# Modulation sums moved from VectorE to GpSimd, with a shorter expert choice and another order of the filling blocks, in a fused two-block kernel

## The chip, the cores and the metric

One Trainium2 chip (trn2), one of its cores. The metric is the device time in microseconds of one execution; lower is better. The kernel before took 1738.4 us, the median of 3 runs (1738.04 to 1740.64).

## What is computed

256 tokens (SEQ), width 1024, float32 throughout. The first block has four layers, each with another mixer; every layer is modulated by a condition vector `c`:

```python
cond = jax.nn.silu(c)
for i in range(DEPTH):                      # 4 layers: gla, sgu, fox, gla
    mod = (cond @ w_mod[i] + b_mod[i])[:, None, :]
    shift, scale, gate = jnp.split(mod, 3, axis=-1)
    h = rms_norm(x, norm_pre_g[i]) * (1.0 + scale) + shift
    o = mixer(h)                            # w_in, mixing, w_out
    x = x + gate * rms_norm(o, norm_post_g[i])
```

The second block adds a hybrid mixer (three attention groups, a convolution, gates) and then the PEER feed-forward: for each token and each of 8 heads the 16 best of 128 x 128 experts, found from two sets of 128 scores, whose rows of `expert_down` and `expert_up` are gathered from HBM:

```python
top_s, top_i = lax.top_k(s, 16)             # per head: 16 best keys of each of two sets
best_s, pos = lax.top_k(cand_s, 16)         # of the 256 sums
idx = jnp.take_along_axis(cand_i, pos, axis=-1)          # expert number, key0 * 128 + key1
a = gelu(einsum('cd,ced->ce', x, expert_down[idx]))
y = einsum('ce,ced->cd', softmax(best_s) * a, expert_up[idx])
```

## The kernel before, in words

The tokens are two tiles of 128 (t = 0 and 1). All engines run one list, `ORDER`, which `make_order` writes out: each engine walks it and does its share of every step, so an engine that waits at a step holds everything behind it on that engine. The steps of tile 0 set the order. A `"gap"` in the lists of chunks stands where tile 0 has to wait for a chain of small work; the next block of tile 1 is put there to fill TensorE. A block is one `("mm", t, name, i)`: 8 matmuls of 128x512 (line 948) from 2 MB of weights that SP loads into a ring of four 1 MB places. Tile 1 is behind tile 0 and its last layers run beside the expert gathers of tile 0.

**Modulation.** A layer's shift, scale and gate are three vectors of 1024. `w_mod` of a layer is read in 24 pieces of 128x1024 (three thirds of KC = 8 pieces). The piece, times one column of `cond`, is added to a running sum of 128x1024; afterwards a matmul with ones adds up the 128 partitions. `PIECES` lists the 96 pieces. Pieces 0 to 15 (shift and scale of layer 0) are loaded by SP at the start, two at a time, into `early`. Six of them (`PE_PIECES`) are done by TensorE itself in `piece_columns` (line 986), the other ten by VectorE in `add_piece` (line 1567). The other 80 come over GpSimd's queue (`fetch`, line 849) into the four places of `mring`, and VectorE adds each of them at a `("mod", n)` step; `pieces_at` says how many such steps stand behind each block. `start_sums` (lines 856 and 857) clears the three sums of a layer and loads the bias, `fetch_post` loads `norm_post_g`. There are two sets of sums, for even and odd layers.

The sums are read by TensorE at `mod_cols` of a layer (line 1010: 8 matmuls for the shift and 8 for the scale, before the layer's first block) and at `mod_gate` (line 1019, behind the fifth and sixth block of the layer). The evacuation of the first block of layer 3 by ScalarE waits for all 96 pieces, since its target lies where `mring` and the sums lie.

**The start.** TensorE: `piece_columns` of pieces 5 and 7, the transposes of both tiles (line 927), `piece_columns` of pieces 9, 11, 13, 15, then `mod_cols` 0, then the first block.

**Fox layer** (layer 2): eight blocks; `forget_sum` (line 1100), `quad_T` (line 1111), `quad_S` (line 1123) are the steps behind its blocks 3 and 4. After the output projection of each of the layers there are two filling blocks.

**Experts.** `choose` makes the 16 picks of a head on VectorE (lines 1732 to 1781). 256 picks in all (PICKS), 128 per tile; a `("tick", k)` gathers the rows of pick k on GpSimd (line 877), takes the dot product with the down row on VectorE (line 1798) and adds the weighted up row of an earlier pick: on VectorE (line 1813) or, through a diagonal matrix made by ScalarE (line 1493), on TensorE (line 1203). `on_vector` says which; `added_at` says at which tick: 18 ticks behind the pick in tile 0 and 6 in tile 1. The weights of tile 1's picks are made in groups of four (`GROUPS`, `weights`, line 1790). `final` adds the two sums and normalizes.

## Time and profile before

| | before |
|---|---|
| median of 3 runs | 1738.4 us (1738.04 to 1740.64) |
| profiled execution, its own time | 1739.41 us |
| span of the profiled execution | 1737.6 us |
| TensorE busy | 1393.7 us, 80% |
| VectorE busy | 1047.5 us, 60% |
| ScalarE busy | 433.1 us, 25% |
| GpSimd busy | 490.7 us, 28% |
| HBM read | 589.55 MB, mean 340 GB/s |

The profile is one execution. Its span lacks 1.8 us of that execution's own time, and that time is 1.0 us above the median. Busy shares are averages over stages which have different limits, so they are read by stage: the layers (0 to about 800 us), the time in which tile 1's layers run beside tile 0's gathers (to about 1390 us), and the gathers of tile 1.

### The profile page before, as it was taken

To read this page: it belongs to the slowest core of one execution; us is meant where nothing else is said; L and a number is where in the kernel's file an instruction comes from. 1 tells how busy PE (TensorE), PEld (TensorE's weight loads), DVE (VectorE), ACT (ScalarE), POOL (GpSimd) and SP (SyncE) were. 2 spreads that over 40 slices of the span, in tenths; PEclk is the share of its full clock that TensorE was granted. 3 is DMA by queue.
4 is the path that set the end of the run, shared out by engine and by line. 5 is a ranking of instruction groups with operands and counts; after the bars stand their busy time and mean duration, and the time that the engine had idled before them with its cause. 6 is when DMAs were issued, how large, how long until landed. Compare 5 with 4: busy or idle time off the path is not lost. (4 is left out here: it accounts for less than half of the span.)

```text
span 1737.6 us, 13867 instructions
## 1 busy us (share of the span) xinstructions
PE 1393.7 (80%) x4158; PEld 717.6 (41%) x4158; DVE 1047.5 (60%) x2197; ACT 433.1 (25%) x974; POOL 490.7 (28%) x498
## 2 busy tenths in 40 slices
PE   6998988978999999999777777699787647666665
PEld 6454435444444455444354343455333312222222
DVE  3645554553233222313797998788866778877876
ACT  1221413423423421102133232132002221111111
POOL 2101210210000000000445546355344545444441
PEclk9998998989999999999897888798888878898898
DMA  9978884978556776887999989999999999999995
GB/s 386 377 256 303 312 340 171 347 282 295 213 207 219 277 265 242 290 293 265 402 361 357 413 339 403 412 400 413 410 414 414 348 412 422 421 422 421 422 421 248
DMA packets 108941, 591.53 MB, mean 340 GB/s; under 512 B 12450, under 2 KB 12706, under 8 KB 60612
## 3 DMA queue, kind: packets, MB, share of 16 engines
q0 software_dynamic: 67776, 312.56, 45.4%
q1 hardware_dynamic: 41092, 278.10, 42.2%
q8 instruction: 34, 0.56, 0.1%
q14 instruction: 39, 0.32, 0.0%
HBM read 589.55 MB, written 1.05 MB: 340 GB/s over the span
## 5 line engine op out<-in xcount | busy, mean ns | idle before, releaser
L948 PE MATMUL bank<-ring,hT 128*128 128x512 f32 x1888 | 866.6, 615 | 39.6 <-DVE room L1920 12.1
L948 PEld LDWEIGHTS bank<-ring,hT 128*128 128x128 f32 x1888 | 366.5, 198 | 482.2 <-issue 449.8
L877 POOL DMA_INDIRECT room<-in_peer_down,idx x92 | 102.5, 1114 | 525.1 <-DVE idx L1781 401.8
L1798 DVE CUSTOM_DVE_ANT_0 room<-room 128x1024 f32<-128x1024 f32 x180 | 218.6, 1221 | 50.6 <-DMA room<-in_pair,idx 38.4
L1203 PE MATMUL bank<-room 128*128 128x512 f32 x284 | 150.9, 676 | 96.5 <-ACT room L1493 94.2
L1813 DVE SCALAR_TENSOR_TENSOR x<-room,pcoef,x 128x1024 f32<-128x1024 f32 x121 | 155.7, 1287 | 28.0 <-DMA room<-in_peer_up,idx 27.5
L877 POOL DMA_INDIRECT room<-in_peer_up,idx x104 | 114.0, 1096 | 88.6 <-DVE pa L1798 42.3
L1203 PEld LDWEIGHTS bank<-room 128*128 128x128 f32 x284 | 57.5, 215 | 190.8 <-issue 97.2
L849 POOL DMA_DIRECT2D room<-in_w_mod x80 | 42.2, 528 | 326.3 <-DVE room L1567 206.5
L877 POOL DMA_INDIRECT room<-in_pair,idx x88 | 97.0, 1102 | 108.5 <-PE bank L1203 50.6
L927 PE MATMUL bank<-cst,room 128*128 128x128 f32 x424 | 64.7, 297 | 55.3 <-ACT room L1439 24.1
L1203 PE MATMUL bank<-ring,room 128*128 128x512 f32 x116 | 72.6, 774 | 38.0 <-ACT room L1493 38.0
L1567 DVE SCALAR_TENSOR_TENSOR room<-room,cst 128x1024 f32<-128x1024 f32 x58 | 74.4, 1282 | 36.0 <-DMA room<-in_w_mod 26.8
L927 PEld LDWEIGHTS bank<-cst,room 128*128 128x128 f32 x424 | 54.9, 153 | 82.4 <-ACT room L1439 26.8
L964 PE MATMUL bank<-room 128*128 128x128 f32 x256 | 43.9, 331 | 34.7 <-DVE room L1592 34.7
L1493 ACT ACTIVATE room<-cst,pcoef 128x128 f32<-128x128 f32 x102 | 36.8, 392 | 118.0 <-DVE pcoef L1790 110.8
L1439 ACT ACTIVATE room<-room,anm 128x128 f32<-128x128 f32 (+1 forms) x80 | 35.4, 443 | 116.3 <-DVE anm L2004 116.3
L877 POOL DMA_INDIRECT ring<-in_pair,idx x40 | 46.6, 1166 | 61.8 <-PE bank L1203 30.8
L1798 DVE CUSTOM_DVE_ANT_0 ring<-ring,room 128x1024 f32<-128x1024 f32 x40 | 48.8, 1226 | 23.1 <-DMA ring<-in_pair,idx 22.8
L1203 PEld LDWEIGHTS bank<-ring,room 128*128 128x128 f32 x116 | 26.7, 243 | 80.6 <-ACT room L1493 52.3
L964 PEld LDWEIGHTS bank<-room 128*128 128x128 f32 x256 | 40.0, 236 | 44.9 <-DVE room L1592 40.1
L1272 ACT ACTIVATE room<-bank 128x512 f32<-128x512 f32 x24 | 14.3, 596 | 147.0 <-PE bank L948 147.0
(304 smaller groups left out, 1527.4 us busy)
## 6 DMA issues: line engine op xcount, KB each, us to landing
ring<-in_wpk SPq DMA_DIRECT2D x248, 1024.0 KB, 7.0
room<-in_w_mod POOLq DMA_DIRECT2D x80, 512.0 KB, 8.2
room<-in_w_mod SPq DMA_DIRECT2D x8, 1024.0 KB, 15.8
room<-in_norm_post_g POOLq DMA_DIRECT2D x4, 512.0 KB, 5.0
rowb<-in_gate_bias SPq DMA_DIRECT2D x4, 512.0 KB, 9.0
room<-in_peer_up,idx POOLq DMA_INDIRECT x104, 12.5
room<-in_peer_down,idx POOLq DMA_INDIRECT x92, 12.4
room<-in_pair,idx POOLq DMA_INDIRECT x88, 14.3
```

Of the source, the lines that this page charges most:

```text
L849: pool.dma_start(mring[n % 4], w[:, k, third * D:(third + 1) * D]).then_inc(S(f"pool_in{n % 4}"), 16)
L877: return pool.indirect_dma_start(out=dst, out_offset=None, in_=A[table][0] if table != "pair" else A[table], in_offset=bass.IndirectOffset ...
L927: last = tr(cols4(b, i), src(i), ident)
L948: last = mm(bank[p][:, :], lhs, ring[:, h % 4, k * N:(k + 1) * N], start=(kk == 0), stop=(h == halves[-1] and k == 3))
L964: last = mm(cols4((b, c, a)[l % 3], h), k_[:, h * P:(h + 1) * P], q_[:, h * P:(h + 1) * P], start=True, stop=True)
L1203: last = mm(bank[WORK[tile][i]][:, :], diag[:, nth % 4, :], row[:, i * N:(i + 1) * N], start=(v == mine[0]), stop=(v == mine[-1]), skip_gr ...
L1272: af(dst, src, ACT.Copy).then_inc(done, 1)
L1439: last = af(s, s, ACT.Exp, bias=anm[:, t, n, h:h + 1], accum_out=al[:, t, n, h:h + 1])
L1493: af(diag[:, nth % 4, :], ident, ACT.Copy, scale=pcoef[:, v // TOPK % 4, v % TOPK:v % TOPK + 1]).then_inc(S("diag"), 1)
L1567: v.scalar_tensor_tensor(out=a, in0=piece, scalar=const("cond", k, 1), in1=a, op0=ALU.mult, op1=ALU.add).then_inc(S("summed"), 1)
L1798: v.tensor_tensor_reduce(out=row, in0=row, in1=u_(g // MINE), scale=1.0, scalar=0.0, op0=ALU.mult, op1=ALU.add, accum_out=pa[:, g // TOPK ...
L1813: v.scalar_tensor_tensor(out=x[:, tile, :], in0=row, scalar=pcoef[:, w, e:e + 1], in1=x[:, tile, :], op0=ALU.mult, op1=ALU.add) \
```

## The change

It does seven things.

1. The 80 pieces behind layer 0's shift and scale (`POOL_PIECES`) are multiplied and added by GpSimd, in two instructions each (a tensor_tensor in place in `mring`, and one into the sum), and the `("mod", n)` steps and `pieces_at` are gone. GpSimd adds one piece after the other, four loads ahead, and counts them in `pool_summed`; TensorE's and ScalarE's waits for pieces are now waits for that count. The first load waits until VectorE has done its part of the first 16.
2. Of the first 16 pieces TensorE does two (5 and 7), VectorE fourteen.
3. The fox layer has a filling block behind its block 3, and only one behind its output projection.
4. In tile 0's query projection the transpose and the scores of the first two heads stand one block earlier, and so does `choose` 0.
5. `choose` has fewer instructions: the two casts to float go, the pairs of comparisons, products and sums are one instruction each, and the last product writes the integer index itself.
6. The last eight picks' up rows are added two to a tick, the last group of four weights is two groups of two, and VectorE and TensorE share these rows otherwise; four ticks fewer.
7. The semaphores `wsT` and `gqk` are one, `dve_set`.

```diff
 def out_chunks(t, L):
     return [([("gated_T", t, L)], ("mm", t, f"out{L}", 0), [("post0", t, L)]),
             ([], ("mm", t, f"out{L}", 1), [("post1", t, L)]),
-            "gap twice"]
+            "gap" if L == 2 else "gap twice"]
...
             b(3, [], [("unit", t, 1), ("forget_sum", t)]),
+            "gap",
             b(4, [], [("quad_T", t, 0), ("quad_S", t, 0)]),
...
-            b(0, name="query", pre=[("norm_in", t, 5)]),
-            b(1, [("score_T", t, 0)], name="query"),
-            b(2, [("score_S", t, 0), ("score_T", t, 1)], name="query"),
+            b(0, [] if t else [("score_T", t, 0)], name="query", pre=[("norm_in", t, 5)]),
+            b(1, [("score_T", t, 0)] if t else [("score_S", t, 0)], name="query"),
+            b(2, ([("score_S", t, 0)] if t else []) + [("score_T", t, 1)], name="query"),
...
-TICKS = PICKS + REST + LEAD[1]
-PIECES = [(L, third, k) for L in range(DEPTH) for third in range(3) for k in range(KC)]
-
-PE_PIECES = (5, 7, 9, 11, 13, 15)
-
...
-def summed_before(n):
+TICKS = PICKS + REST + 2
+
+
+FIRST = [(0, third, k) for third in range(2) for k in range(KC)]
+PE_PIECES = (5, 7)
+DVE_FIRST = len(FIRST) - len(PE_PIECES)
+POOL_PIECES = [(0, 2, k) for k in range(KC)] \
+    + [(L, third, k) for L in range(1, DEPTH) for third in range(3) for k in range(KC)]
+
+
+def first_before(n):
     return n - sum(i < n for i in PE_PIECES)
 
...
+def shifts_of(L):
+    return KC * (3 * L - 1)
...
+def scales_of(L):
+    return KC * 3 * L
...
+def gates_of(L):
+    return KC * (3 * L + 1)
...
 def on_vector(u):
-    return u < 7 * TOPK or u % 4 == 3 or (u % 2 and (u < MINE or u >= PICKS - 8))
+    return u < 7 * TOPK or (u % 4 == 3 and u < PICKS - 4) or (u % 2 and u < MINE) \
+        or u >= PICKS - 2 or (u % 2 and PICKS - 8 <= u < PICKS - 4)
...
 def added_at(v):
+    if v >= PICKS - 8:
+        return tick_of(PICKS - 2) + (v - PICKS + 8) // 2
     return tick_of(v) + LEAD[v // MINE]
...
-ADDS = {added_at(v): [v] for v in range(PICKS)}
+ADDS = {k: [v for v in range(PICKS) if added_at(v) == k] for k in range(TICKS)}
...
-GROUPS = [(hh * TOPK, TOPK) for hh in range(PH)] + [(MINE + 4 * m, 4) for m in range(MINE // 4)]
+GROUPS = [(hh * TOPK, TOPK) for hh in range(PH)] + [(MINE + 4 * m, 4) for m in range(MINE // 4 - 1)] \
+    + [(PICKS - 4, 2), (PICKS - 2, 2)]
...
-        for _ in range(pieces_at(mm)):
-            if piece < len(PIECES):
-                order.append(("mod", piece))
-                piece += 1
...
-            if name == "query" and n == 2:
+            if name == "query" and n == 1:
                 order.append(("choose", 0))
-                rows.tick()
-            if name == "query" and n == 3:
-                rows.tick()
-                rows.tick()
+            if name == "query" and n >= 2:
+                for _ in range(n - 1):
+                    rows.tick()
     order += pending
...
+            def fetch(i):
+
+                if i >= len(POOL_PIECES):
+                    return
+                if i >= 4:
+                    pool.wait_ge(S("pool_summed"), i - 3)
+                pool.dma_start(mring[i % 4], piece_of(*POOL_PIECES[i])).then_inc(S(f"pool_in{i % 4}"), 16)
+
+            def add_piece(i):
+                L, third, k = POOL_PIECES[i]
+                pool.wait_ge(S(f"sums_init{L % 2}"), sums_set(L))
+                pool.wait_ge(S(f"pool_in{i % 4}"), (i // 4 + 1) * 16)
+                link(nc.gpsimd.tensor_tensor(mring[i % 4], mring[i % 4], const("cond", k, 1).to_broadcast([P, D]), ALU.mult))
+                if i:
+                    pool.wait_ge(S("pool_summed"), i)
+                nc.gpsimd.tensor_tensor(sums[L % 2][third], sums[L % 2][third], mring[i % 4], ALU.add) \
+                    .then_inc(S("pool_summed"), 1)
+                fetch(i + 4)
...
-            for n in range(2 * KC, len(PIECES)):
-                fetch(n)
-                if n % (3 * KC) == 3 * KC // 2 and n > 3 * KC:
-                    fetch_post(n // (3 * KC))
-                if n in (6 * KC - 1, 9 * KC - 1):
-                    start_sums((n + 1) // (3 * KC))
+            pool.wait_ge(S("summed"), DVE_FIRST)
+            for i in range(4):
+                fetch(i)
+            for i in range(len(POOL_PIECES)):
+                if i in (gates_of(1), gates_of(2)):
+                    start_sums(i // (3 * KC) + 1)
+                    fetch_post(i // (3 * KC))
+                add_piece(i)
+            fetch_post(DEPTH - 1)
...
-            for piece in PE_PIECES[:2]:
+            for piece in PE_PIECES:
...
-                    if L == 0:
-                        for piece in PE_PIECES[2:]:
-                            piece_columns(piece, p)
...
-                        if j % KC == 0:
-                            pe.wait_ge(S("summed"), summed_before(L * 3 * KC + j + KC))
+                        if j == 0 and L:
+                            pe.wait_ge(S("pool_summed"), shifts_of(L))
+                        elif j == 0:
+                            pe.wait_ge(S("summed"), first_before(KC))
+                        elif j == KC:
+                            pe.wait_ge(S("pool_summed") if L else S("summed"), scales_of(L) if L else DVE_FIRST)
...
-                    pe.wait_ge(S("summed"), summed_before((L + 1) * 3 * KC))
+                    pe.wait_ge(S("pool_summed"), gates_of(L))
...
                         if L == 3 and t == 0 and i == 0:
-                            act.wait_ge(S("summed"), summed_before(len(PIECES)))
+                            act.wait_ge(S("pool_summed"), gates_of(DEPTH - 1))
...
+            def add_first(n):
+                _, third, k = FIRST[n]
...
+                    dve.wait_ge(S("sums_init0"), sums_set(0))
+                dve.wait_ge(S(early_in(n // 2)), 16)
+                a = sums[0][third]
+                v.scalar_tensor_tensor(out=a, in0=early[n // 2][:, n % 2, :], scalar=const("cond", k, 1), in1=a,
...
-                    v.tensor_copy(pixf[:, :, :], pix[:, :, :])
...
-                    link(v.tensor_copy(pabf[:, :, :], pab[:, :, :]))
                 elif part == 2:
-                    for c in range(2):
-                        last = v.tensor_tensor(hot[:, c, :, :], const("iota").unsqueeze(1).to_broadcast([P, TOPK, TOPK]),
-                                               pabf[:, c, :].unsqueeze(2).to_broadcast([P, TOPK, TOPK]), ALU.is_equal)
-                    link(last)
-                    for c in range(2):
-                        last = v.tensor_tensor(hot[:, c, :, :], hot[:, c, :, :],
-                                               pixf[:, c, :].unsqueeze(1).to_broadcast([P, TOPK, TOPK]), ALU.mult)
-                    link(last)
+                    both = [P, 2, TOPK, TOPK]
+                    link(v.tensor_tensor(hot, const("iota").unsqueeze(1).unsqueeze(1).to_broadcast(both),
+                                         pab[:, :, :].unsqueeze(3).to_broadcast(both), ALU.is_equal))
+                    link(v.tensor_tensor(hot, hot, pix[:, :, :].unsqueeze(2).to_broadcast(both), ALU.mult))
                 else:
-                    for c in range(2):
-                        last = v.tensor_reduce(psel[:, c, :], hot[:, c, :, :], X, ALU.add)
-                    link(last)
-                    link(v.scalar_tensor_tensor(out=pidf[:, :], in0=psel[:, 0, :], scalar=float(NK), in1=psel[:, 1, :],
-                                                op0=ALU.mult, op1=ALU.add))
+                    link(v.tensor_reduce(psel[:, :, :], hot, X, ALU.add))
                     if 4 <= hh < PH + 4:
                         for u in range((hh - 4) * TOPK, (hh - 3) * TOPK):
                             if u in PE_NTH:
                                 _, landed, count = landed_row("up", u)
                                 dve.wait_ge(landed, count)
-                    v.tensor_copy(idx[:, w, :], pidf[:, :]).then_inc(S("picked"), 1)
+                    v.scalar_tensor_tensor(out=idx[:, w, :], in0=psel[:, 0, :], scalar=float(NK), in1=psel[:, 1, :],
+                                           op0=ALU.mult, op1=ALU.add).then_inc(S("picked"), 1)
...
```

GpSimd's queue from its last small load on. Before, the pieces are loads alone (x21, x11 and so on, with `norm_post_g` and the clearing of sums between):

```order
19 L857 DMA skT<-in_b_mod 1x16x64
20 L863 DMA room<-in_norm_post_g 128x1024
21 L849 DMA room<-in_w_mod 128x1024 x21
22 L863 DMA room<-in_norm_post_g 128x1024
23 L849 DMA room<-in_w_mod 128x1024 x11
```

And with the change, whose first rows are these:

```order
20 L882 DMA room<-in_norm_post_g 128x1024
21 L857 DMA room<-in_w_mod 128x1024 x4
22 L863 ISA
23 L863 TENSOR_TENSOR room<-room,cst 128x1024
24 L866 TENSOR_TENSOR room<-room 128x1024
25 L857 DMA room<-in_w_mod 128x1024
26 L863 TENSOR_TENSOR room<-room,cst 128x1024
27 L866 TENSOR_TENSOR room<-room 128x1024
```

Two instructions over 128x1024 and one load make a piece, and the three follow one another on this one queue, 80 times; one ISA instruction stands ahead of the first.

TensorE around the fox layer's forget_sum (line 1100 before) and the first query and key transposes (line 1111 before), in the kernel before:

```order
66 L927 MATMUL bank<-cst,room 128x128 x8
67 L948 MATMUL bank<-ring,hT 128x512 x16
68 L1100 MATMUL bank<-lowg,cst 128x16
69 L948 MATMUL bank<-ring,hT 128x512 x8
70 L1111 MATMUL bank<-cst,room 66x128 x8
71 L1123 MATMUL bank<-room 128x128 x4
```

The same place with the change (lines 1123, 970 and 1134 are lines 1100, 948 and 1111 of before):

```order
65 L949 MATMUL bank<-cst,room 128x128 x8
66 L970 MATMUL bank<-ring,hT 128x512 x16
67 L1123 MATMUL bank<-lowg,cst 128x16
68 L970 MATMUL bank<-ring,hT 128x512 x16
69 L1134 MATMUL bank<-cst,room 66x128 x8
70 L1146 MATMUL bank<-room 128x128 x4
```

One more block of 8 matmuls lies between the sum and the transposes; the block it is taken from stood behind the `mod_cols` of layer 3.

## Rows read from the trace of the kernel before

**Rows 1.** Windows by stage: PE, PEld, DVE, ACT, POOL busy us, PEclk, DMA share, GB/s

```profile
50.00:450.00 400.00, 347.31 (x1104) 185.32 (x1103) 206.07 (x355) 121.83 (x261) 49.88 (x90) 0.92 0.79 293
450.00:800.00 350.00, 335.54 (x1016) 166.95 (x1015) 88.51 (x232) 86.00 (x190) 0.00 (x0) 1.00 0.72 254
800.00:825.00 25.00, 23.43 (x91) 13.14 (x90) 9.01 (x39) 6.13 (x11) 2.90 (x3) 1.00 0.79 271
...
1400.00:1700.00 300.00, 187.40 (x337) 71.04 (x336) 241.13 (x576) 58.42 (x151) 134.39 (x121) 0.86 1.01 421
```

**Rows 2.** Timeline of the start: start us, us, engine, line, operation, idle before

```profile
23.11 2.60 DVE L1567 SCALAR_TENSOR_TENSOR room<-room,cst 128x1024 f32<-128x1024 f32 x2
...
25.49 13.65 PE L986 MATMUL bank<-cst,room 128*128 128x1 f32 x64
...
29.20 1.28 DVE L1567 SCALAR_TENSOR_TENSOR room<-room,cst 128x1024 f32<-128x1024 f32 x1 [1.27 <-DMA room<-in_w_mod]
...
39.00 6.97 PE L1010 MATMUL bank<-ones,room 128*128 128x1 f32 x32
...
47.79 8.50 PE L948 MATMUL bank<-ring,hT 128*128 128x512 f32 x16 [1.82 <-DVE hT L1859]
```

**Rows 3.** Timeline of TensorE, 80 to 502 us

```profile
84.48 3.58 PE L964 MATMUL bank<-room 128*128 128x128 f32 x16 [2.49 <-DVE room L1592]
...
148.15 2.25 PE L1010 MATMUL bank<-ones,room 128*128 128x1 f32 x16
155.41 9.31 PE L948 MATMUL bank<-ring,hT 128*128 128x512 f32 x16 [5.00 <-DVE room L1920]
...
232.68 2.08 PE L1019 MATMUL bank<-skT,ones 128*128 128x512 f32 x2 [5.72 <-DVE gateb L1839]
234.55 8.92 PE L948 MATMUL bank<-ring,hT 128*128 128x512 f32 x16
...
287.54 3.63 PE L1010 MATMUL bank<-ones,room 128*128 128x1 f32 x32
...
464.26 7.11 PE L948 MATMUL bank<-ring,hT 128*128 128x512 f32 x16 [1.19 <-DVE hT L1859]
...
499.60 1.16 PE L964 MATMUL bank<-room 128*128 128x128 f32 x8 [2.54 <-DVE room L1592]
```

**Rows 4.** TensorE's waits, 300 to 400 us: us in total, times, longest

```profile
PE bank L1123 <- DVE room L1986: 7.1, 2, 4.4
PE bank L1111 <- DVE room L1977: 2.8, 1, 2.8
PE bank L1100 <- DVE lowg L1971: 2.3, 1, 2.3
```

**Rows 5.** Groups by line, GpSimd and VectorE's additions: busy us, mean ns, idle before, releaser

```profile
L1567 DVE SCALAR_TENSOR_TENSOR room<-room,cst 128x1024 f32<-128x1024 f32 x58 | 74.4, 1282 | 36.0 <-DMA room<-in_w_mod 26.8 <-DMA room<-in_b_mod 8.0
...
L856 POOL MEMSET room<- 128x1024 f32 x8 | 7.8, 970 | 0.0
L857 POOL DMA_DIRECT2D room<-in_b_mod x8 | 4.2, 520 | 2.4 <-POOL room L856 2.4
```

**Rows 6.** The page, section 6: issues, KB each, median us from issue to landing

```profile
room<-in_w_mod POOLq DMA_DIRECT2D x80, 512.0 KB, 8.2
```

**Rows 7.** Timeline of the first choice on VectorE

```profile
811.26 0.49 DVE L1732 MAX8 pv<-room 128x8 f32<-128x128 f32 x2 [10.83 <-ACT room L1474]
...
817.61 0.76 DVE L1763 TENSOR_TENSOR room<-cst,pabf 128x256 f32<-128x256 f32 x2
```

**Rows 8.** Timeline of the end, from the last dot product on

```profile
1722.75 1.22 DVE L1798 CUSTOM_DVE_ANT_0 room<-room 128x1024 f32<-128x1024 f32 x1 [1.21 <-DMA room<-in_pair,idx]
...
1724.57 5.42 PE L1203 MATMUL bank<-room 128*128 128x512 f32 x12 [1.20 <-ACT room L1493]
...
1725.27 4.03 DVE L1813 SCALAR_TENSOR_TENSOR x<-room,pcoef,x 128x1024 f32<-128x1024 f32 x3
...
1730.02 1.28 DVE L2086 TENSOR_TENSOR x<-x,bank 128x512 f32<-128x512 f32 x2 [0.72 <-PE bank L1203]
```

More of the change, by code:

```diff
@@ L289 @@
 EXP_AT = {sums_at(hh): hh for hh in range(T * PH) if hh != PH - 1}
-GROUPS = [(hh * TOPK, TOPK) for hh in range(PH)] + [(MINE + 4 * m, 4) for m in range(MINE // 4)]
+GROUPS = [(hh * TOPK, TOPK) for hh in range(PH)] + [(MINE + 4 * m, 4) for m in range(MINE // 4 - 1)] \
+    + [(PICKS - 4, 2), (PICKS - 2, 2)]
 GROUP_AT = {tick_of(g + n - 1) + 1: i for i, (g, n) in enumerate(GROUPS)}
 def group_of(v):
-    return v // TOPK if v < MINE else PH + (v - MINE) // 4
+    return next(i for i, (g, n) in enumerate(GROUPS) if g <= v < g + n)
 WAY = {"norm_in": 110, "low": 10, "decay": 12, "qk_T": 15, "level": 25, "cross": 30, "heads": 80, "gated_T": 50,
@@ L367, in make_order @@
             second.append(c)
-    done, pending, ahead, piece = 0, [], False, 2 * KC
+    done, pending, ahead = 0, [], False
     for c in first:
@@ L843, in _, with piece_of @@
             nc.gpsimd.memset(alT[:, :], 1.0).then_inc(S("ones_set"), 1)
-            def fetch(n):
-                L, third, k = PIECES[n]
-                pool.wait_ge(S("summed"), summed_before(2 * KC if n < 2 * KC + 4 else n - 3))
-                w = A["w_mod"][L].rearrange("(p k) n -> p k n", k=KC)
-                pool.dma_start(mring[n % 4], w[:, k, third * D:(third + 1) * D]).then_inc(S(f"pool_in{n % 4}"), 16)
+            def piece_of(L, third, k):
+                return A["w_mod"][L].rearrange("(p k) n -> p k n", k=KC)[:, k, third * D:(third + 1) * D]
+            def fetch(i):
[14 more added lines that the diff above has]
+                fetch(i + 4)
             def start_sums(L):
@@ L980, in piece_columns @@
             def piece_columns(n, p):
-                _, third, k = PIECES[n]
+                _, third, k = FIRST[n]
                 pe.wait_ge(S(early_in(n // 2)), 16)
@@ L1088, in _ @@
                     pe.wait_ge(S(f"ln{t}"), 2)
-                    pe.wait_ge(S("wsT"), 1)
+                    pe.wait_ge(S("dve_set"), 1)
                     for g in range(SG):
@@ L1546, in copy_half @@
                     .then_inc(S(f"a_T{t}"), 1)
-            def add_piece(n):
-                L, third, k = PIECES[n]
+            def add_first(n):
+                _, third, k = FIRST[n]
                 if n in PE_PIECES:
@@ L1553, in add_piece @@
                     dve.wait_ge(S("shift_init"), 16)
-                elif n % (3 * KC) == 0 or n == KC:
-                    dve.wait_ge(S(f"sums_init{L % 2}"), sums_set(L))
-                if n == 0:
                     dve.wait_ge(S("cond"), 1)
                 else:
-                    dve.wait_ge(S("summed"), summed_before(n))
-                a = sums[L % 2][third]
-                if n < 2 * KC:
-                    piece = early[n // 2][:, n % 2, :]
-                    dve.wait_ge(S(early_in(n // 2)), 16)
-                else:
-                    piece = mring[n % 4]
-                    dve.wait_ge(S(f"pool_in{n % 4}"), (n // 4 + 1 - KC // 2) * 16)
-                v.scalar_tensor_tensor(out=a, in0=piece, scalar=const("cond", k, 1), in1=a,
+                    dve.wait_ge(S("summed"), first_before(n))
+                if n == KC:
+                    dve.wait_ge(S("sums_init0"), sums_set(0))
+                dve.wait_ge(S(early_in(n // 2)), 16)
+                a = sums[0][third]
+                v.scalar_tensor_tensor(out=a, in0=early[n // 2][:, n % 2, :], scalar=const("cond", k, 1), in1=a,
                                        op0=ALU.mult, op1=ALU.add).then_inc(S("summed"), 1)
@@ L1828, in _ @@
                     for n in range(KC if L == 0 else 0):
-                        add_piece(KC + n)
+                        add_first(KC + n)
                     src, done = produced(dve, *step)
@@ L1978, in _ @@
                     if t == 0:
-                        v.tensor_tensor(gqk[:, :], const("gq"), const("gk"), ALU.mult).then_inc(S("gqk"), 1)
+                        v.tensor_tensor(gqk[:, :], const("gq"), const("gk"), ALU.mult).then_inc(S("dve_set"), 1)
                 elif kind == "quad_T" and t == 0:
```

25 lines of the change are left out of this document (7 added, 18 removed).

## The prediction, made before the change ran

> **What bounds the kernel now.** I read the windows by stage first [rows 1]. In the layers TensorE is busy 347 of 400 us, then 336 of 350, while the DMA engines move 293 and 254 GB/s. In the gathers of tile 1 they move 421 GB/s, all 16 busy. So the layers are a matter of TensorE and of what it waits for, the end is a matter of bytes, and what the layers gain or lose moves the start of the gathers and so the end, nearly one for one. The second view is TensorE's own timeline [rows 3], to be read for its brackets: there stand its waits, and most name VectorE. The question is which come from the 80 pieces. The level step at 84.48 waits 2.49 us with additions in VectorE's queue; the same step of layer 3, at 499.60, has none there and waits 2.54. So the waits in the levels stay. The wait of 5.00 us at 155.41, of 5.72 at 232.68 and the 12.2 us of the fox layer (7.1 + 2.8 + 2.3) [rows 4] stand where additions of 1.28 us each, three or more in a row, lie in VectorE's queue; these can shrink. Behind such a wait the next block takes 8.92 or 9.31 us instead of 7.11 [rows 3], as the granted clock falls.
>
> **The start.** TensorE's last 32 of six pieces' 48 matmuls take 13.65 us, and then the 16 of mod_cols 6.97 [rows 2]. With the change those 32 go. VectorE has eight additions instead of four from 23.11 on, two of them in 2.60 us; the last data was there at 29.20. 23.1 + 8 x 1.30 = 33.5. Then the scale half, 3.5 us, to 37.0, instead of 46.0: the first block comes 9 us earlier. What hides VectorE's four more additions is nothing; they are in this sum.
>
> **GpSimd's pieces** are the term on which all hangs. A piece is a product and a sum over 128x1024, a load to issue at 0.52 us, and two waits on itself, each 0.30 us as before the small loads (2.4 us over 8) [rows 5]. For the two instructions, w each, the trace has no row. Below they are bounded by GpSimd's memset of the same size, 0.97 us, which only writes [rows 5]; above by three such passes, one for each operand and one for the result, 2.91. I take two passes, 1.94: two operands through one stream, with the writing beside; VectorE's 1.28 for its own addition lies between and says only that one pass is too little. Then a piece takes 2 x 1.94 + 0.52 + 0.60 = 5.0 us. The first load is issued at 33.8 and lands 8.2 us later [rows 6], at 42. So piece n is in at 42 + 5.0 n, and 6 us later behind each of the two places where sums are cleared and a row loaded (3 x (0.97 + 0.30 + 0.52) + 0.5), at 32 and at 56.
>
> Now the deadlines, by TensorE's times of before [rows 3]. *Layer 1's scale*, 24 pieces: 162 us. Its 8 matmuls started at 148.15. TensorE would be there at 141 (the start's 9 us less 2, since the constants behind the first weights land late) and waits 21 us; the net loss is 14. The wait of 5.00 behind it is filled, so +9. *The gate of layer 1*, 32 pieces: 202, in time; its 5.72 us and the slow block behind (1.8) go: +1.5. The other waits between shrink by about 2: -0.5. *Layer 2's scale*, 48 pieces: 288; TensorE is there at 289.4 - 0.5 (half of the 3.63 from 287.54), just in time. *Fox*: of 12.2 us I take half, since VectorE's own work and the change of banks stay, and 2 of slow clock: -8.5. The added filling block helps there and costs 7.1 us ahead of layer 3's mod_cols, which it takes out behind: nothing in sum. *All 80*: 42 + 400 + 12 = 454, before the first block of layer 3 ends (464.26 + 7.1). Nothing waits.
>
> **The rest.** The first scores are made one block earlier, 7 us, and the choice is some 0.7 us shorter (two casts and one more; three pairs of 128x256, 0.76 us the pair [rows 7], become one instruction of what I estimate at 0.69). So gathers start 8 us earlier, in a stretch at 271 GB/s of 421 [rows 1]: 8 x (1 - 271/421) = 2.8 us of transfer, less 0.8 for TensorE's wait on an evacuation: -2. Fifteen more choices save 10 us of VectorE under the transfers; I take -1. *The end*: after the last dot product TensorE had three rows, 5.42 us, VectorE three, 4.03 [rows 8]. Now TensorE has two, 3.6 us, and VectorE three that it starts 0.1 us later: its first addition in parallel with the gelu, two behind. The final addition starts at about 1728.4 instead of 1730.0: -1.6.
>
> **Sum**: -0.5 - 8.5 - 2 - 1 - 1.6 = -13.6, against the profiled execution's own 1739.4: 1725.8; that execution was 1.0 above the median, so 1725. The 9 us of the start are inside, spent on the wait for layer 1's scale.
>
> The Trainium skill, GPSIMD Engine Reference, section Performance versus the Vector engine, gives 4497 ns for a tensor_tensor of 2048 float32 on GpSimd, because both operands come through one read port; half of it is 2.25 us for 1024. By that page the sum would be the second rival's; no row here shows a GpSimd instruction that reads.
>
> **The rivals.**
> *Cheap GpSimd.* At w = 0.97 to 1.4 a piece takes 3.1 to 3.9 us, 24 are in at 116 to 136, and nobody waits. Then the start's 7 us stay, the 5.0 shrinks to 2, and with -7.5, -2, -8.5 and -4.6 it is about -33: 1706. Against it: an instruction with two operands at a memset's price or little above.
> *GpSimd sets the pace.* From w = 2.1 on the pieces are behind all the way. At 2.25 a piece takes 5.6 us: layer 1's scale at 177 (+29, after the filled wait +24), -9.5 to the next, 48 pieces at 318 where TensorE is at 304 (+29, less 3 of a wait behind it), -8.5 through fox, +17; all 80 at 502 us, where the evacuation stands at 488 and a block covers 7: +24 there. With -4.6 behind: 1758. Each 0.1 us of w costs 16 us more, since 80 pieces with two instructions each stand in the queue; at 2.91 it is about 1860. What speaks for it: 80 pieces in 430 us leave 5.3 us each, and mine have 5.0. It turns slower at w = 2.05. By the Trainium skill's figure above this is the case that comes.
> *VectorE and GpSimd in each other's way.* VectorE's level steps are tensor_tensors with two operands in SBUF. If one has to wait while GpSimd reads, it is half a GpSimd instruction, 1 us, and up to four times in each of the 14 levels of layer 0: 56 us, of which I let TensorE see a third, +19. With 0.3 us more for each piece (+24 over 80, of which my sum has 17 in hand at the last deadline and none at layer 2's scale, +14) it is 1755 to 1790. The trace cannot show it, as GpSimd reads nothing in it. The Trainium skill, SBUF — State Buffer, section Who interferes with whom, states just this: a VectorE instruction with two SBUF inputs and a GpSimd instruction that reads SBUF shut each other out for their whole length.
> *No gain*: the sizes cancel, 1738.
>
> **Chances.** Forecast (1712 to 1735) 0.38, cheap 0.15, GpSimd's pace 0.29, in each other's way 0.12, no gain 0.06. A measurement tells 0.2% from no change, 3.5 us. Faster: 0.38 + 0.15 less a little, 0.52; same 0.06; slower 0.42. The range leaves out the far end of slow GpSimd and the lowest of the cheap one: 1702 to 1775. The forecast's own range is 1712 to 1735.
>
> **What would show it.** Right: GpSimd's two instructions at 1.9 us, starts of pieces 5.0 us apart; TensorE in the first block at 39 to 40; one wait of some 20 us before layer 1's scale matmuls, and none over 3 us for GpSimd behind it; fox waits halved; the final addition 6 us behind the last dot product instead of 7.3. Wrong: waits for GpSimd's sums before layer 2's scale or layer 3's first evacuation (then w is over 2.05), none before layer 1's (then under 1.4), or, in the layers, VectorE's two-operand instructions over 128x256 longer than the 0.4 us that two of them, 0.76 together, take now [rows 7].

## The result and the profile after

The changed kernel takes **1798.48 us** (median of 4 runs, 1796.05 to 1801.71) where the kernel before took 1739.52 beside it (4 runs, 1738.04 to 1743.54): the ratio is 1.0336, with a 95% interval of 1.0312 to 1.0361. 1725 was forecast, with 1702 to 1775 as the range. It is slower by 59 us, beyond the far end.

The page's sections 1 and 2 of the kernel after:

```profile
span 1795.9 us, 13817 instructions
PE 1400.2 (78%) x4094; PEld 713.9 (40%) x4094; DVE 1108.1 (62%) x2026; ACT 436.0 (24%) x977; POOL 850.8 (47%) x658
PE   5878785877889999999987866889787746666765
DVE  5676695364313322321578898689784868878776
POOL 3999899899500000000345554555542564444542
```

VectorE gave away 80 additions of 1.28 us and took on four, a net 97 us, and is busy *longer* than before: 1108.1 us against 1047.5. Something made its other instructions longer, by some 150 us. In slices 2 to 10 GpSimd is busy for 80% and more of the time, and TensorE is at 50 to 80%, where it was at 70 to 90% and more before.

Was GpSimd late? Its groups from 50 to 480 us (busy us, mean ns of one, idle before):

```profile
L863 POOL TENSOR_TENSOR room<-room,cst 128x1024 f32<-128x1024 f32 x78 | 148.9, 1910 | 4.1 <-DMA skT<-in_b_mod 2.0 <-DMA room<-in_b_mod 0.9
L866 POOL TENSOR_TENSOR room<-room 128x1024 f32<-128x1024 f32 x47 | 114.3, 2432 | 3.7
```

The product takes 1.91 us, the sum 2.43: the forecast's two passes of 1.94 were close. The pieces start 5.3 us apart where 5.0 was forecast, and the last sum ended at about 475 us, not 454. TensorE's timeline answers to [rows 2, 3]:

```profile
38.68 9.86 PE L970 MATMUL bank<-ring,hT 128*128 128x512 f32 x16 [1.82 <-DVE hT L1865]
...
166.07 3.57 PE L1033 MATMUL bank<-ones,room 128*128 128x1 f32 x16 [2.98 <-POOL room L866]
...
332.55 3.63 PE L1033 MATMUL bank<-ones,room 128*128 128x1 f32 x32
...
429.90 2.08 PE L1042 MATMUL bank<-room,ones 128*128 128x512 f32 x2 [5.46 <-ACT room L1300]
...
486.35 9.60 PE L970 MATMUL bank<-ring,hT 128*128 128x512 f32 x16 [5.15 <-DVE hT L1567]
...
525.48 7.11 PE L970 MATMUL bank<-ring,hT 128*128 128x512 f32 x16 [1.19 <-DVE hT L1865]
```

The first block starts at 38.68 (47.79 before, 38.8 forecast). Layer 1's scale was forecast at 162 behind a wait of 21 us; it comes at 166.07, but the wait for GpSimd is 2.98. TensorE itself came there at 163, 22 us behind the 141 at which the forecast had it. Layer 2's sums are read at 332.55 (287.54 before, +45), layer 3's first block runs at 525.48 (464.26, +61), and the end is 58 us later. TensorE has no second wait for GpSimd. From its waits from 0 to 850 us (us in total, times, longest), after and then before:

```profile
PE bank L986 <- DVE room L1609: 56.5, 14, 7.9
...
PE bank L949 <- DVE room L1559: 12.5, 3, 10.7
```

```profile
PE bank L964 <- DVE room L1592: 18.7, 11, 3.1
```

L986 are the matmuls of a level of gated linear attention (L964 before). Ahead of each level stand four short VectorE instructions, tensor_tensors of 128x256: two differences, and behind ScalarE's exponentials two products, which the matmuls read. L1609 is the last of the four. These four after, with two others below them, from 50 to 480 us (ns: least, median, most), and the last of them before:

```profile
L1598 DVE TENSOR_TENSOR room<-room x14: 414/1841/2550, 69.5 to 299.2; 128x256 f32<-128x256 f32 x14
L1599 DVE TENSOR_TENSOR room<-room x14: 410/2486/2571, 71.2 to 301.1; 128x256 f32<-128x256 f32 x14
L1607 DVE TENSOR_TENSOR room<-room x14: 410/687/2561, 76.5 to 307.0; 128x256 f32<-128x256 f32 x14
L1609 DVE TENSOR_TENSOR room<-room x14: 410/2552/2566, 76.8 to 309.2; 128x256 f32<-128x256 f32 x14
L1618 DVE COPY_PREDICATED room<-gmask,bank x16: 712/723/731, 84.6 to 313.9; 128x512 f32<-128x512 int32 x16
L1847 DVE TENSOR_TENSOR gateb<-bank,room x6: 678/692/693, 104.4 to 446.5; 128x512 f32<-128x512 f32 x6
```

```profile
L1592 DVE TENSOR_TENSOR room<-room x14: 414/418/420, 84.0 to 269.1; 128x256 f32<-128x256 f32 x14
```

From 0.42 us, never over 0.43, to a median of 2.55 for the last. L1618 and L1847, which take one operand from a bank of PSUM (`room` is SBUF), stay at their length. The two timelines of the same 5 us, VectorE and then GpSimd, tell why:

```profile
299.24 1.95 DVE L1598 TENSOR_TENSOR room<-room 128x256 f32<-128x256 f32 x1
301.11 0.41 DVE L1599 TENSOR_TENSOR room<-room 128x256 f32<-128x256 f32 x1
301.44 2.56 DVE L1607 TENSOR_TENSOR room<-room 128x256 f32<-128x256 f32 x1
```

```profile
298.48 2.42 POOL L866 TENSOR_TENSOR room<-room 128x1024 f32<-128x1024 f32 x1
301.20 0.59 POOL L857 DMA_DIRECT2D room<-in_w_mod  x1 [0.30 <-POOL room L866]
301.80 1.91 POOL L863 TENSOR_TENSOR room<-room,cst 128x1024 f32<-128x1024 f32 x1
```

L1598 starts inside GpSimd's sum and ends at 301.19, 0.29 us behind its end (300.90). L1599 falls into the pause in which GpSimd issues a load, and takes 0.41. L1607 ends at 304.00, again 0.29 behind the product's end (303.71), although its row starts 0.36 us before the product's. In these rows a GpSimd instruction of 2 us holds a VectorE instruction of 0.4.

### The profile page after: what moved, and what is told of

Same layout as the page of the kernel before. It is cut to its first block and busy times, and to the rows that moved or that the text cites. A ratio compares the mean times of both kernels' runs of the same rounds, so it can differ in the third digit from the quotient of the medians.

```text
span 1795.9 us, 13817 instructions
## 1 busy us (share of the span) xinstructions
PE 1400.2 (78%) x4094; PEld 713.9 (40%) x4094; DVE 1108.1 (62%) x2026; ACT 436.0 (24%) x977; POOL 850.8 (47%) x658
## 5 line engine op out<-in xcount | busy, mean ns | idle before, releaser
L970 PE MATMUL bank<-ring,hT 128*128 128x512 f32 x1888 | 875.7, 620 | 39.5 <-DVE room L1926 7.4
L970 PEld LDWEIGHTS bank<-ring,hT 128*128 128x128 f32 x1888 | 370.4, 200 | 488.2 <-issue 461.2
L1806 DVE CUSTOM_DVE_ANT_0 room<-room 128x1024 f32<-128x1024 f32 x180 | 219.0, 1222 | 58.3 <-DMA room<-in_pair,idx 41.6
L1226 PE MATMUL bank<-room 128*128 128x512 f32 x284 | 157.5, 703 | 95.7 <-ACT room L1516 93.6
L899 POOL DMA_INDIRECT room<-in_peer_up,idx x104 | 121.9, 1172 | 87.8 <-DVE pa L1806 45.6
L863 POOL TENSOR_TENSOR room<-room,cst 128x1024 f32<-128x1024 f32 x80 | 152.7, 1909 | 9.0 <-DMA room<-in_w_mod 4.9
L899 POOL DMA_INDIRECT room<-in_pair,idx x88 | 101.5, 1153 | 111.0 <-PE bank L1226 58.6
L1226 PEld LDWEIGHTS bank<-room 128*128 128x128 f32 x284 | 60.2, 224 | 191.9 <-issue 100.4
L866 POOL TENSOR_TENSOR room<-room 128x1024 f32<-128x1024 f32 x48 | 116.6, 2430 | 3.8
L986 PE MATMUL bank<-room 128*128 128x128 f32 x256 | 47.5, 345 | 72.6 <-DVE room L1609 72.5
L1226 PE MATMUL bank<-ring,room 128*128 128x512 f32 x116 | 66.4, 716 | 40.0 <-ACT room L1516 40.0
L986 PEld LDWEIGHTS bank<-room 128*128 128x128 f32 x256 | 42.4, 247 | 83.8 <-DVE room L1609 79.0
L857 POOL DMA_DIRECT2D room<-in_w_mod x80 | 46.3, 579 | 43.7 <-DVE room L1584 21.2
L1462 ACT ACTIVATE room<-room,anm 128x128 f32<-128x128 f32 (+1 forms) x80 | 35.4, 443 | 110.2 <-DVE anm L2010 110.2
## 6 DMA issues: line engine op xcount, KB each, us to landing
room<-in_peer_down,idx POOLq DMA_INDIRECT x92, 13.6
```

The source lines that it names most:

```text
L857: pool.dma_start(mring[i % 4], piece_of(*POOL_PIECES[i])).then_inc(S(f"pool_in{i % 4}"), 16)
L863: link(nc.gpsimd.tensor_tensor(mring[i % 4], mring[i % 4], const("cond", k, 1).to_broadcast([P, D]), ALU.mult))
L866: nc.gpsimd.tensor_tensor(sums[L % 2][third], sums[L % 2][third], mring[i % 4], ALU.add) \
L899: return pool.indirect_dma_start(out=dst, out_offset=None, in_=A[table][0] if table != "pair" else A[table], in_offset=bass.IndirectOffset ...
L970: last = mm(bank[p][:, :], lhs, ring[:, h % 4, k * N:(k + 1) * N], start=(kk == 0), stop=(h == halves[-1] and k == 3))
L986: last = mm(cols4((b, c, a)[l % 3], h), k_[:, h * P:(h + 1) * P], q_[:, h * P:(h + 1) * P], start=True, stop=True)
```

## The experiments

Twelve kernels ran. *Theory*: VectorE's instructions with two operands in SBUF wait for the end of a GpSimd instruction that reads there. *Rivals*: GpSimd's pace and the order of the pieces; the filling block or another small part. A ratio is to the kernel before, measured beside the run (1742 to 1744 us, 3 to 4 us above its time beside the changed kernel, so ratios compare better than times), and brackets hold its 95% interval. Runs 3, 5, 9 and 10 leave the modulation's sums out, so they are for timing alone.

**1. VectorE adds, the rest as changed.** The diff against the kernel before is that of the change without its hunks on the pieces (`POOL_PIECES`, `DVE_FIRST`; `pieces_at` and the `("mod", n)` steps stay), and with `PE_PIECES = (5, 7)`.

> The changed kernel with part 1 undone: VectorE keeps the 80 additions, all else (matrix pieces, fox filler, query, shorter choice, tail) as changed. Theory (all that was lost comes from GpSimd's pieces): the start's 9 us are partly kept, tail 1.7, choices 2 to 3: 1720 to 1732 us, 8 to 18 below the kernel before. Rival (another part, such as the filling block or the choice, costs much of it): above 1745. VectorE's two-operand instructions at 0.41 to 0.43 us in the layers.

1736.48 us (10 runs) against 1742.23 (15): ratio 0.9958 [0.9931, 0.9986]. VectorE is busy 1043.8 us. The whole loss is GpSimd's part, but the gain, 0.4% or 6 to 7 us, is under the expected 8 to 18.

**2. GpSimd adds, the rest as before.** The changed kernel with the hunks on gaps, query, choice and end undone.

> The kernel before with part 1 alone: GpSimd adds the 80 pieces. Theory: it has the whole loss and none of the small gains of the choice and the tail: 1795 to 1812 us, with TensorE's waits for the levels' merges near 56 us up to 850 us. Rival (the parts together are what costs): below 1770.

1788.67 us: 1.0256 [1.0207, 1.0305]. The levels' wait is 51.5 us. The loss is there, but below the expected 1795 to 1812 us: it is 10 us less than in the changed kernel (14 by the ratios), where the other parts should have taken time off. Runs 11 and 12 take that up.

**3. GpSimd only writes.**

```diff
-link(nc.gpsimd.tensor_tensor(mring[i % 4], mring[i % 4], const("cond", k, 1).to_broadcast([P, D]), ALU.mult))
+for _ in range(2):
+    link(nc.gpsimd.memset(mring[i % 4], 0.0))
...
-nc.gpsimd.tensor_tensor(sums[L % 2][third], sums[L % 2][third], mring[i % 4], ALU.add) \
-    .then_inc(S("pool_summed"), 1)
+link(nc.gpsimd.memset(mring[i % 4], 0.0))
+nc.gpsimd.memset(sums[L % 2][third], 0.0).then_inc(S("pool_summed"), 1)
```

> The changed kernel with each GpSimd piece (product and sum, 1.91 + 2.35 us) replaced by four memsets of the tile, near 3.9 us in all, with the same transfers behind: the sums of the modulation are left out. It keeps GpSimd busy at nearly the same pace and order, without its two-operand reads. Theory (a GpSimd instruction with two operands in SBUF keeps VectorE's two-operand instructions waiting): VectorE's levels at 0.42 us, TensorE's wait for them back near 19 us, 1710 to 1728 us. Rival 1 (GpSimd's pace and the order of pieces cost it): within 10 us of 1798. Rival 2 (any GpSimd access to SBUF, writes too, holds VectorE): levels still above 1 us, over 1770.

1729.3 us: 0.9921 [0.9892, 0.995], 1 us above the expected 1710 to 1728. GpSimd is busy almost as long (806.5 us for 850.8), with a piece each 4.8 us instead of 5.3. VectorE has the same 2026 instructions:

```profile
PE 1384.4 (80%) x4094; PEld 702.8 (41%) x4094; DVE 955.8 (56%) x2026; ACT 435.5 (25%) x977; POOL 806.5 (47%) x818
```

```profile
L1610 DVE TENSOR_TENSOR room<-room x14: 418/421/423, 78.7 to 266.5; 128x256 f32<-128x256 f32 x14
```

```profile
155.04 3.57 PE L1034 MATMUL bank<-ones,room 128*128 128x1 f32 x16 [13.13 <-POOL room L868]
```

The levels are at 0.42 and the wait for them is 17.5 us, near the 18.7 of before. 1108.1 - 955.8 = **152 us** is what VectorE was held beyond run 3, and the execution is 69 us longer (72 by the ratios). Those 69 us hold the piece's 0.5 us of slower pace too; run 9, at the pace of the changed kernel, takes that up. The wait for GpSimd at layer 1's scale, 2.98 us in the changed kernel, is here 13.1: TensorE arrives on time again, and GpSimd is the late one. GpSimd's presence and its writes are ruled out as the cause of the long levels; its reads are left.

The writes are not free for every instruction. VectorE's `tensor_scalar` of the norm, SBUF to SBUF with one tensor operand, in the kernel before and in run 3:

```profile
L1536 DVE TENSOR_SCALAR room<-x,rstd x8: 478/484/489, 159.9 to 454.3; 128x512 f32<-128x512 f32 x8
L1560 DVE TENSOR_SCALAR room<-x,rstd x8: 468/638/1461, 164.1 to 451.7; 128x512 f32<-128x512 f32 x8
```

Not all of the loss is waiting. Up to the first gather the changed kernel (876.6 us) and run 3 (806.0) do the same 2245 matmuls (PE, PEld, DVE, ACT, POOL busy us, PEclk, DMA share, GB/s):

```profile
0.00:876.60 876.60, 733.86 (x2245) 386.60 (x2246) 392.47 (x572) 224.41 (x484) 412.64 (x275) 0.92 0.73 261
0.00:806.00 806.00, 710.00 (x2245) 372.43 (x2246) 240.30 (x572) 223.99 (x484) 367.78 (x434) 0.95 0.78 284
```

TensorE, which waits more, has a lower mean granted clock, and 24 of the 71 us of delay are longer matmuls.

**4. Each GpSimd instruction in four quarters** (both run over `[:, q]`, q of 256 columns, for j in 0 to 3).

> The changed kernel with each GpSimd product and sum cut into four instructions of 128x256. Theory A (VectorE waits until the GpSimd instruction in progress ends): VectorE's longest two-operand instruction falls from 2.57 to about 1.1 us, TensorE's wait for the levels from 56 to about 30 us, and the time to 1765 to 1785 us. Theory B (the two share the access, whatever the length): longest and mean as in the changed kernel, 1795 to 1810 us.

1828.21 us: 1.0483 [1.0439, 1.0526], slower, against theory A's time. What the two theories differ on came out as A says:

```profile
L1606 DVE TENSOR_TENSOR room<-room x14: 410/942/947, 69.5 to 304.9; 128x256 f32<-128x256 f32 x14
L1616 DVE TENSOR_TENSOR room<-room x14: 410/884/949, 76.0 to 308.5; 128x256 f32<-128x256 f32 x14
```

```profile
PE bank L1040 <- POOL room L872: 65.5, 2, 44.7
PE bank L993 <- DVE room L1616: 29.1, 12, 4.5
```

The most is 0.95 us, not 2.57, and the wait for the levels 29.1 (about 30 expected). The time went elsewhere. A quarter takes 0.63 us (product) and 0.76 (sum), so a piece costs 5.5 us instead of 4.3 in instructions alone, and TensorE waits 65.5 us for GpSimd. The expectation left that out. In L1605 and L1614 single instructions still took 2.36 and 2.96 us. The one of 2.96 starts at 78.05 and ends at 81.01, 0.30 us behind four quarters in a row (78.39 to 80.71): VectorE was passed over at each of their ends.

**5 and 6. A scalar product.** In run 6 the product is `tensor_scalar` by the column of `cond`; run 5 does that twice and replaces the sum by a memset.

```diff
-link(nc.gpsimd.tensor_tensor(mring[i % 4], mring[i % 4], const("cond", k, 1).to_broadcast([P, D]), ALU.mult))
+link(nc.gpsimd.tensor_scalar(mring[i % 4], mring[i % 4], const("cond", k, 1), None, ALU.mult))
```

> The changed kernel with each GpSimd piece made of two products by a per-partition scalar (one operand read in SBUF each, the second a repeat that keeps GpSimd reading) and one memset of the sum: the sums of the modulation are left out. Theory A (any GpSimd instruction that reads SBUF holds VectorE's instructions with two operands there): VectorE's levels far above 0.42 us, their maximum near the length of one product. Theory B (it takes a GpSimd instruction with two operands in SBUF): levels at 0.42 us throughout, time within 8 us of the one with memsets alone (1729).

> The changed kernel with the product of each piece as a multiplication by a per-partition scalar in place of a second, broadcast operand; the sum as it was. If the broadcast operand sets the product's 1.91 us, the product falls to 1.0 to 1.3 us, the share of GpSimd's time that holds VectorE from 4.3 of 5.2 us to about 3.5 of 4.4, and the time to 1775 to 1790 us. If not, 1.9 us and 1795 to 1801 us.

Run 5: 1945.28 us, 1.1154 [1.1132, 1.1176]; run 6: 1823.29 us, 1.0451 [1.0429, 1.0472]. Neither of the two expected prices came: the form with fewer operands is the *slower* one, 2.85 us against 1.91 (run 6's row):

```profile
L863 POOL TENSOR_SCALAR room<-room,cst x80: 2839/2852/3498, 40.7 to 551.1; 128x1024 f32<-128x1024 f32 x80
```

Both times are in the main GpSimd's pace (TensorE waits 58.3 us for it in run 6, 157.4 at one line in run 5) and say little of the holding. VectorE's rows do. In run 5, two of the four levels' instructions:

```profile
L1599 DVE TENSOR_TENSOR room<-room x14: 409/414/422, 69.3 to 337.2; 128x256 f32<-128x256 f32 x14
L1609 DVE TENSOR_TENSOR room<-room x14: 411/417/1440, 76.6 to 340.0; 128x256 f32<-128x256 f32 x14
```

Most pass at 0.42 though GpSimd reads 72% of the time (2 x 2.86 us in each 8.0), and a few take up to 1.77 (L1598, not shown). That is neither theory A nor B as written: this form holds VectorE now and then. Why it lets most pass is open.

**7 and 8. The start's part alone.** Run 7 is run 1 with six `PE_PIECES`, run 8 the kernel before with `PE_PIECES = (5, 7)`.

> The kernel before with the filling block, the earlier query and choice, and the shorter end, VectorE adding all pieces and the six matrix pieces kept. If the start's 9 us are swallowed by the wait for layer 1's scale, as forecast, it lies with the one that has the start too (0.9958 of the kernel before): 0.994 to 0.998. If the start gives most of that gain, 0.998 to 1.001.

> The kernel before with two matrix pieces (5 and 7) in place of six, VectorE adding the rest, nothing else changed. Swallowed: TensorE's first block 9 us earlier, layer 1's scale at 144 against 146.5, and 0.998 to 1.000 of the kernel before. Kept: 0.995 to 0.997.

Run 7: 1737.81 us, 0.996 [0.994, 0.998]. Run 8: 1739.51 us, 0.9979 [0.9959, 0.9999]. With the other parts present the start adds nothing that can be told (0.9958 and 0.996). Run 8's interval holds values of both its cases, so its time doesn't decide between them. Alone it moves the matmuls on layer 1's sums from 146.45 to 142.56 and the first gather from 821.2 to 814.8. So 9 us become 4 to 6, and in the end about 4 (0 to 7 by the interval).

**9 and 10. Only the sum, only the product.** Run 9 has two memsets for the product, run 10 three for the sum.

> The changed kernel with each piece's product replaced by two memsets (1.9 us, writes alone) and the sum of two tensors kept: what is summed is zero, so the modulation's sums are left out. GpSimd's pace stays at 5.2 us a piece. Theory (VectorE's instruction waits for the end of the GpSimd instruction that reads two tensors): VectorE's levels bimodal, 0.42 us and up to 2.57 us (sum 2.35 and its own), and the time between memsets alone (1729) and the changed kernel (1798), by the share of the held time 2.35 of 4.26: 1760 to 1775 us. Rival (it takes the product with its broadcast operand): 1725 to 1740.

> The changed kernel with each piece's product kept and its sum replaced by three memsets (2.9 us, writes alone, near the sum's 2.35): the sums are left out. Theory: VectorE's levels bimodal with a maximum near 2.1 us (product 1.91 less what has run, and its own 0.42), time 1750 to 1768. Rival (only two whole tensors hold VectorE, a broadcast column doesn't): levels at 0.42, 1725 to 1740.

Run 9: 1754.9 us, 1.0061 [1.0039, 1.0083], below the expected 1760 to 1775. Run 10: 1791.81 us, 1.0276 [1.0259, 1.0294], above the expected 1750 to 1768. First the longest on VectorE: both hold it, as the theory had it, though run 10's 2.45 us is above its 2.1 (run 9, then run 10).

```profile
L1608 DVE TENSOR_TENSOR room<-room x14: 407/426/2574, 76.2 to 282.1; 128x256 f32<-128x256 f32 x14
L1610 DVE TENSOR_TENSOR room<-room x14: 405/413/420, 78.5 to 284.0; 128x256 f32<-128x256 f32 x14
```

```profile
L1610 DVE TENSOR_TENSOR room<-room x14: 412/418/2445, 76.2 to 293.0; 128x256 f32<-128x256 f32 x14
```

Then where the time is (run 9, then run 10):

```profile
PE bank L1034 <- POOL room L867: 25.1, 1, 25.1
PE bank L987 <- DVE room L1610: 22.8, 12, 3.6
```

```profile
PE bank L1034 <- POOL room L868: 54.4, 2, 37.8
PE bank L987 <- DVE room L1610: 20.5, 10, 3.4
```

The waits for the levels do **not** share out by held time. 18.7 us before, 22.8 with the sum alone, 20.5 with the product alone, 56.5 with both. VectorE's own time in the four instructions says the same: 35.4 us in run 9 and 33.2 in run 10, against 23.4 before and 93.4 with both. The rows let one read why. The four stand in two pairs, L1599 and L1600, L1608 and L1610 (run 9's lines). Each alone leaves 2 to 3 us of memsets in every piece, and the second of a pair follows there: in run 9 L1599 and L1608 are held (up to 2.24 and 2.57 us), L1600 and L1610 never. (In run 10 its L1610 is held at times, up to 2.45 us, but its median is 0.42.) With both, the open stretches of a piece are the 0.9 us around the issue and 0.08 between the two instructions, and the second of a pair is the one most held (medians of 2.49 and 2.55 us, 1.84 and 0.69 for the first).

Run 10's time is in the main pace: three memsets are 2.9 us against the sum's 2.43, and a piece comes every 5.8 us. Run 9 has the changed kernel's 5.3 and is 44 us faster (48 by the ratios), so the pace alone doesn't make the loss. It shows the forecast's own picture: a wait of 25.1 us ahead of layer 1's scale (21 forecast, at 162; here 168.03).

**11 and 12. The filling block in the fox layer, undone.** Run 11 undoes it in the changed kernel, run 12 in run 1.

```diff
-            "gap" if L == 2 else "gap twice"]
+            "gap twice"]
...
-            "gap",
             b(4, [], [("quad_T", t, 0), ("quad_S", t, 0)]),
```

> The changed kernel with the filling block back behind the layer's output product instead of in the fox layer. If that move costs the changed kernel its 10 us over GpSimd alone (1788.7), since VectorE's slower norm chain there has lost its cover: 1786 to 1792. If not: 1796 to 1806.

> The first experiment (VectorE adds, 0.9958 of the kernel before) with the filling block put back behind the layer's output product. By the two profiles the move takes some 11 us of wait from the fox layer's small products and brings two of 5.2 and 5.5 us behind the output product of the layer before: it should be worth 0 to 2 us, so 0.995 to 0.998 here. If the move costs as much as it did in the changed kernel (13 us): 0.988 to 0.991.

Run 11: 1785.31 us, 1.0255 [1.0234, 1.0277], so the block costs the changed kernel 13 us (14 by the ratios); the time is just below the expected 1786 to 1792. Run 12: **1731.29 us, 0.9939 [0.992, 0.9957]**, the fastest kernel that computes all. Its interval overlaps run 1's, 0.9931 to 0.9986, and lies between the two cases of its expectation: what the block costs there is 3 us by the ratios, not settled. From the waits of TensorE from 300 to 850 us, run 1 and then run 12:

```profile
...
PE bank L949 <- DVE hT L1545: 6.0, 3, 5.1
PE bank L1020 <- ACT room L1278: 5.5, 1, 5.5
...
PE bank L1124 <- DVE room L1978: 4.2, 2, 3.2
```

```profile
PE bank L1123 <- DVE room L1977: 6.7, 2, 3.6
...
PE bank L1111 <- DVE room L1968: 1.6, 1, 1.6
```

The filler does take waits out of the fox layer. It leaves two, of 5.5 us ahead of the layer's output product and of 5.1 behind it, and tile 0's first gather comes at 815.7 in run 1 and at 808.4 in run 12 (821.2 before). In the changed kernel it has less to fill: without it (run 11) the fox layer's three waits are 2.2, 2.0 and 0.9 us, since no addition stands in VectorE's queue there, and with it 3.8 us in all. So it saves 1.3 us of waits there, uncovers the same two, and the first gather comes at 876.6 instead of 862.2.

## Why the prediction was wrong

**The step that failed** is "So the waits in the levels stay", and with it the sum, in which the 80 additions leave VectorE and nothing else there changes: it has no term for what GpSimd's reads do to the instructions that stay. The levels' waits went from 18.7 to 56.5 us, VectorE was held for 152 us, and the execution took 59 us more, not 14 less. The third rival named this mechanism and its place, the levels. It got 0.12 and a price of 1755 to 1790, and the result lies above it. By its own steps:

- *56 us more in 14 levels of layer 0.* Measured: 93.4 us for the 56 instructions (31.1 + 22.8 + 20.8 + 18.7) against 56 x 0.418 = 23.4, so 70 us, more than the 56. "Half a GpSimd instruction" was too little for the last one: it starts as soon as its predecessor is let go, just when GpSimd's next instruction starts, and waits for all of it.
- *TensorE sees a third, 19 us.* It saw 56.5 - 18.7 = 38 us, over half.
- *Only the levels were counted.* More than half of the hold lay elsewhere: 152 us in all, 70 in the levels. The norm ahead of the transposes (L1559) takes 0.47 us at best and 1.98 at the median, and at 385.39 TensorE waits 10.7 us for a chain of held instructions that ends in it (neither the kernel before nor run 3 has a wait there). Even an addition of 128x1 (L1548, 0.16 us) took up to 2.33 us:

```profile
L1559 DVE TENSOR_SCALAR room<-x,rstd x6: 469/1978/2662, 184.9 to 385.3; 128x512 f32<-128x512 f32 x6
L1548 DVE TENSOR_TENSOR rstd<-rstd,newt x11: 159/166/2334, 142.7 to 414.9; 128x1 f32<-128x1 f32 x7, 128x4 f32<-128x4 f32 x2, 128x16 f32<-128x16 f32 x2
```

- *0.3 us more for each piece.* The product stayed at 1.91, the sum went from 2.34 at least to 2.43 on the mean: GpSimd hardly pays, VectorE does.
- *The clock* had no term either: 24 us of the delay up to the first gather are matmuls at a lower granted clock.

The Trainium skill, SBUF — State Buffer, section Who interferes with whom, says that a VectorE instruction with two SBUF inputs contends with a GpSimd instruction that reads SBUF and not with one that only writes it, and that this is an exclusive lock. The trace agrees: 2.55 us against 0.42 with writes alone, and 0.95 with quarters. The rival was given 0.12, with the remark that the trace could not show it. No row could speak against it either; that, and the 56 such instructions on TensorE's chain that the prediction itself had counted, were reasons to give it more.

**The start** was right: 38.68 for 38.8. That its 9 us are "spent on the wait for layer 1's scale" fits the kernels in which that wait is there: it is 13.1 and 25.1 us in runs 3 and 9. In the changed kernel the hold had taken them before: TensorE comes to layer 1's scale at 163, 15 us later than in the kernel before. Runs 1 and 7, where VectorE adds, have no such wait and yet differ by nothing; why is open.

**GpSimd's price** was near: 1.91 and 2.43 us for 1.94 twice, 5.3 from piece to piece for 5.0. The rival "GpSimd sets the pace", which had 0.29 and gives 1758 at 2.25, did not come: with 2.17 on the mean, above its turning point of 2.05, TensorE never waited for GpSimd behind layer 1's scale, because it was itself 45 us late at layer 2. Runs 4, 6 and 10, with a piece every 6.3, 6.2 and 5.8 us, show how that rival looks: 65.5, 58.3 and 54.4 us of waiting for GpSimd. So the two losses don't add up: in the changed kernel the late TensorE hides GpSimd's pace. Run 3, which writes for about as long as the forecast's two passes (3.83 and 3.88 us), comes to 0.9921, -13 us, where the sum was -13.6. The balance agrees, but its fox term didn't come out, so part of that is luck, and that kernel leaves the sums out.

**Fox, -8.5.** By its own terms, 6.1 and 2, it is -8.1. Its waits went (L1123 2.83, the rest under 1 us, for 12.2 before [rows 4]); run 11, at 5.1 us without the filling block, shows that the half which the forecast took comes from the additions. But that the block costs "nothing in sum" was wrong: without it the changed kernel is 13 us faster. Taken from behind the output product, it uncovered a norm and an evacuation, 5.15 and 5.46 us. Run 1 has the same two at 5.1 and 5.5, so they are not the work of the hold.

**Choice and query, -3.** The first gather went from 814.8 (run 8) to 808.4 (run 12), the parts of the choice and the end being the difference: 6.4 us for 8 forecast. In time these parts give 0.9979 to 0.9939, 7 us for the 4.6 forecast, with intervals of 3 us and more either way. With GpSimd adding they can't be seen: run 2, without them, is at 1.0256 and run 11 at 1.0255. **The end, -1.6**, was right: from the last dot product (1782.71) to the final addition (1788.30) are 5.6 us where there were 7.3 [rows 8].

```profile
1782.71 1.22 DVE L1806 CUSTOM_DVE_ANT_0 room<-room 128x1024 f32<-128x1024 f32 x1
...
1784.57 3.70 PE L1226 MATMUL bank<-room 128*128 128x512 f32 x8 [1.26 <-ACT room L1516]
...
1788.30 1.29 DVE L2092 TENSOR_TENSOR x<-x,bank 128x512 f32<-128x512 f32 x2 [0.20 <-PE bank L1226]
```

## What to carry to other kernels

Before tensor work moves from VectorE to GpSimd, list VectorE's instructions on the critical chain that take two operands from SBUF, however small: each can wait for a whole GpSimd instruction (here 0.42 us became 2.55), while TensorE's chain hangs on it. Busy time is the first sign: here the engine that lost 97 us of work was busier than before. If work must go there, open stretches between GpSimd's reading instructions help (with 2 us of writes in between the waits for the levels were 22.8 us instead of 56.5), but they cost pace; no run here has such stretches and computes all. Cutting the instructions short didn't pay (run 4). And price a filling block anew when the waits it was meant for have gone.

## What was not expected of the hardware

- The hold's cost doesn't go by the time that GpSimd reads: its two instructions cost the levels 38 us of wait together and 4.1 and 1.8 us singly (runs 9 and 10, at a slower pace in run 10).
- On GpSimd `tensor_scalar` of 128x1024 with a column as its scalar takes 2.85 us, `tensor_tensor` with the same column broadcast 1.91, and the sum of two whole tensors 2.35 (medians). In run 5 `tensor_scalar` held VectorE's two-operand instructions seldom.
- Four instructions of 128x256 take 2.5 us (product) and 3.0 (sum), against 1.91 and 2.35 for one of 128x1024.
- VectorE's `tensor_scalar` from SBUF to SBUF (L1559), with one tensor operand, is held as well, up to 2.66 us, and by GpSimd's writes too: 1.46 us at most in run 3, 0.49 before.
